# Where the split weights of a hybrid decoder layer lie in SBUF: 128 bytes past a 2048-byte multiple, or on it

## The reference, cut to what matters

```python
h = _rmsnorm(x, norm_gain)
proj = h @ w_in                        # (256, 4096) @ (4096, 15416)
(m_q, m_k, m_v, m_o, m_z, m_i, m_f, a_q, ck, cv, sk, sv, wk, wv, a_gate, a_z) = split(proj)
y_m = mlstm(silu(conv(m_q, m_k)), m_v, m_i, m_f) * sigmoid(m_o) ... * silu(m_z)
y_a = nsa(a_q, ck, cv, sk, sv, wk, wv, a_gate, compressor weights, rel_bias) * silu(a_z)
x = x + concatenate([y_m, y_a]) @ w_out      # (256, 4096) @ (4096, 4096)
return _rmsnorm(x, final_norm_gain)
```

## The kernel before, in words

| tile | before, first byte | modulo 2048 |
|---|---|---|
| `lhs_hi`, `lhs_lo` | 16,512 and 49,280 | 128 |
| `w_raw` (16 KiB) | 82,048 | 128 |
| `w_split` (32 KiB) | 98,432 | 128 |
| arena (88,320 bytes; all tiles made by `at`) | 131,200 | 128 |
| `c128` (constants, 444 columns: identity, masks) | 219,520 | 384 |

## Time and profile before

### The profile page before, as it was taken

How to read it: one execution, slowest core, us unless ns; L and a number is a source line. 1 busy time by engine, 2 the same in 40 slices (tenths; PEclk the granted TensorE clock), 3 DMA queues, 4 the chain that set the end, 5 groups by cost and what they waited for, 6 DMA issues and landing times.

```text
span 1848.8 us, 24131 instructions
## 1 busy us (share of the span) xinstructions
PE 1820.6 (98%) x8488; PEld 1511.8 (82%) x8488; DVE 1141.1 (62%) x1461; ACT 828.7 (45%) x1120; POOL 77.1 (4%) x54
## 2 busy tenths in 40 slices
PE   7999999999999999999999999999999999999997
PEld 6878888888888888888888888888888888888886
DVE  4544644467676676876666666756675775455554
ACT  5534444444454444434444444444443544444443
POOL 0000000000101010010000000000000000000000
PEclk9999999999999999999999999999999999999999
DMA  7676555544545444445555556555655566666664
GB/s 266 184 198 208 194 190 192 193 160 149 181 147 171 158 159 160 152 167 172 193 193 188 177 193 193 185 181 194 192 184 181 172 217 237 205 205 204 205 203 172
DMA packets 100266, 345.62 MB, mean 187 GB/s; under 512 B 10932, under 2 KB 16052, under 8 KB 100052
## 3 DMA queue, kind: packets, MB, share of 16 engines
q1 hardware_dynamic: 93448, 332.68, 54.1%
q10 hardware_dynamic: 6736, 11.77, 2.6%
HBM read 337.07 MB, written 7.33 MB: 186 GB/s over the span
## 4 chain that ended last, share of the span: by engine, by line
PE 95%; DMA 2%; ACT 1%; DVE 1%; issue 0%; SPq 0%; POOL 0%; ACTq 0%; DVEq 0%; POOLq 0%
PE acc_a L441 15%; PE acc_b L441 15%; PE acc_a L443 14%; PE acc_a L442 14%; PE acc_b L443 14%; PE acc_b L442 14%; PE bank_v L448 1%; DMA w_raw<-in_w_all 1%; PE bank_z L689 1%; DMA toe_dram<-toe_row 1%; PE bank_x L443 1%; PE bank_x L442 1%; PE bank_x L441 0%; ACT w_split L843 0%; PE bank_v L449 0%
## 5 line engine op out<-in xcount | busy, mean ns | idle before, releaser
L1206 DVE TENSOR_TENSOR w_split<-w_raw,w_split 128x1024 fp32r<-128x1024 f32 x620 | 777.1, 1255 | 599.2 <-ACT w_split L843 596.1
L843 ACT ACTIVATE w_split<-w_raw 128x1024 fp32r<-128x1024 f32 x620 | 655.3, 1059 | 848.9 <-PE acc_a L443 415.2
L441 PE MATMUL acc_a<-w_split,lhs_hi 128*128 128x512 f32 x1216 | 483.3, 397 | 3.2 <-DVE lhs_lo L1275 3.2
L441 PE MATMUL acc_b<-w_split,lhs_hi 128*128 128x512 f32 x1216 | 479.4, 394 | 0.3 <-issue 0.3
L443 PE MATMUL acc_a<-w_split,lhs_lo 128*128 128x512 f32 x1216 | 474.7, 390 | 0.0
L442 PE MATMUL acc_a<-w_split,lhs_hi 128*128 128x512 f32 x1216 | 474.6, 390 | 0.0
L443 PE MATMUL acc_b<-w_split,lhs_lo 128*128 128x512 f32 x1216 | 473.7, 390 | 0.0
L442 PE MATMUL acc_b<-w_split,lhs_hi 128*128 128x512 f32 x1216 | 473.6, 389 | 0.0
L441 PEld LDWEIGHTS acc_a<-w_split,lhs_hi 128*128 128x128 f32 x1216 | 229.0, 188 | 49.2 <-DVE lhs_lo L1275 2.4
L443 PEld LDWEIGHTS acc_a<-w_split,lhs_lo 128*128 128x128 f32 x1216 | 228.7, 188 | 48.7
L443 PEld LDWEIGHTS acc_b<-w_split,lhs_lo 128*128 128x128 f32 x1216 | 228.3, 188 | 48.1
(11 more groups left out here) (274 smaller groups left out, 927.0 us busy)
## 6 DMA issues: line engine op xcount, KB each, us to landing
w_raw<-in_w_all SPq DMA_DIRECT2D x616, 512.0 KB
wide<-in_x SPq DMA_DIRECT2D x8, 512.0 KB, 10.1
xres<-in_x ACTq DMA_DIRECT2D x8, 512.0 KB, 4.3
out_y<-wide SPq DMA_DIRECT2D x8, 512.0 KB, 3.2
toe_dram<-toe_row ACTq DMA_DIRECT2D x4, 766.0 KB, 10.2
toe<-toe_dram ACTq DMA_DIRECT2D x4, 512.0 KB, 4.6
gain_f<-in_final_norm_gain ACTq DMA_DIRECT2D x1, 2048.0 KB, 14.2
w_raw<-in_w_all SPq DMA_DIRECT2D x4, 224.0 KB
```

The costliest lines, as they stand in the source:

```text
L441: pe.matmul(dst, a[0], b[0], start=start, stop=False)
L843: act.activation(w_hi[:, cols], w_raw[:, cols], ACT.Copy).then_inc(hi_done, 1)
L1206: dve.tensor_tensor(w_lo[:, cols], w_raw[:, cols], w_hi[:, cols].bitcast(F32), ALU.subtract).then_inc(lo_done, 1)
```

## The change

A helper `align(n)` is added, which puts an unused tile behind the last one, large enough that the next begins at a multiple of n bytes. `c128` moves from behind the arena to the place behind `lhs_lo`; then comes the gap; then `w_split`; and `w_raw` goes from in front of `w_split` to behind it. No instruction is added, removed or reordered.

```diff
+        def align(n):
+
+            base = (nc.sbuf_base + 31) // 32 * 32
+            if base % n:
+                sb(f"gap_{base}", (n - base % n) // 4)
...
         lhs_lo = sb("lhs_lo", KT_IN * T, F32R)[:, :].rearrange("p (k t) -> p k t", t=T)
-        w_raw = sb("w_raw", RING * 2 * BW)
-
+        c128 = sb("c128", const128.shape[1])
+        align(4 * BW)
         w_split = sb("w_split", 2 * RING * 2 * BW, F32R)[:, :].rearrange("p (s c) -> p s c", s=2)
         w_hi, w_lo = w_split[:, 0], w_split[:, 1]
+        w_raw = sb("w_raw", RING * 2 * BW)
...
-        c128 = sb("c128", const128.shape[1])
         ident = c128[:, 0:P]
```

## The result

The changed kernel takes 1885.75 us as the median of 4 runs (1883.68 to 1887.36), the kernel before 1851.62 us beside it. The ratio is 1.0175, 95% interval 1.0161 to 1.0190. The range of the prediction ended at 1860 us.

The account below looks back on a forecast made before the run. PE's own pace was taken as the bound, 7296 wide matmuls at 226.9 ns each. All terms were taken as 0: 1850.58 + 0 = 1850.6 us, as a median 1852.8 us, range 1842 to 1860 us.

Parts of the forecast that it names:

- the 2.4 us allowed: Weight transfers on the chain, 24.3 us together: a tenth on each would be 2.4 us up or down; taken as 0.
- take the gain back: If the chain's second weight transfer ended earlier, the `toe_dram` copy behind it would take most of the gain back.
- Rival C: DVE's splits grow beyond their 76% slack and PE waits in the attention: +38 us, 1891 us; chance 0.02.
- the rows nearest in kind: Attention matmuls streaming 512 columns, group 0 without and group 3 with 2048-byte crossings, both 0.23 to 0.24 us: term 0.
- T2: Theory of the follow-up experiments: PE's pace hangs on the first byte of the moving operand; slow case 232 ns, 1886 us.
- T1: Theory of the follow-up experiments, the same as Rival B: PE's pace hangs on the distance between its two operands.
- sign for B: In the output projection, a distance over 227.4 ns between starts of PE's matmuls would make Rival B right.
- Rival B: PE's stationary and moving operands no longer share a remainder: +8.1 ns per wide matmul, +59 us, 1912 us; chance 0.06.
- the rows at 235 ns: The slowest steady 512-column rows of PE in the trace, used as the worst case: +8.1 ns per wide matmul.
- Rival A: PE's pace hangs on the moving operand's first byte: up to 13.6 ns per wide matmul back, -99 us, 1754 us; chance 0.10.
- the unexplained 13.6 ns: Part of each 226.9 ns wide-matmul distance beyond 213.3 ns for 512 columns at one a cycle; 99 us in all.

Follow-up runs that it names:

- the layout at 160: The kernel before with a gap of 160 bytes in front of `w_raw`, `lhs` at 128 and the rest at 288 modulo 2048: 1900.82 us, ratio 1.0255.
- the runs with PE alone: Programs without the layer or other engines' work beside PE's stream, 96 matmuls per case, operand addresses or column counts varied: 226.7 ns at equal remainders (128 x 512 columns).
- the first program: Not the layer: PE alone, 22 cases of 96 matmuls of 512 columns with different operand first bytes; 226.7 ns at difference 0, 232.4 or 233.3 at 128.

## Why the prediction was wrong

**Right: what bounds the kernel, and where an edit of addresses could act.** PE's pace over 7296 wide matmuls is where the whole change is.

**Right: the other engines.** DVE's split is at 1224 ns and ACT's at 1046 ns in the fullest stretch, as against 1225 and 1058; the transfer on the chain at 95.62 takes 11.02 us as against 11.85, inside the 2.4 us allowed. The other one, 12.48 us at 9.77, has no counterpart: the chain of the changed kernel runs over PE's matmuls there. The piece behind the second, `toe_dram<-toe_row` (which writes `toe_dram`; the prediction calls it a copy out of it), takes 9.45 us as against 9.82, so it did not take the gain back; with one execution of each, no more can be said. Rival C did not come.

**Wrong: "I take 0, since the rows nearest in kind, with and without the crossing, agree."** The measurement in it was sound, and is still so in the changed kernel: crossing a 2048-byte multiple costs nothing, and neither does a different first byte. The case that the prediction's last line named as the untested one, a moving operand that begins exactly on a multiple of 2048, is fast too as long as `lhs` begins on one (1851.26 and 1851.90 us). But in every row that I compared, both operands of PE lay in the same relation: `q` and `k` lie a multiple of 256 bytes apart, so do `mv` and `sw`, and `w_split` and `lhs`. Those rows varied the first byte and held fixed the one thing that the change altered. They could answer T2 and were blind to T1. The term came out at +5.4 ns per wide matmul (mean of the distances up to 245 ns over the layer: 232.7 against 227.3), 37 us in the sum of all distances, where I had 0. The prediction's own sign for B, a distance over 227.4 ns, is met in every block.

**Rival B had the mechanism and a fair size.** Its price, 8.1 ns from the rows at 235 ns, was 1.5 times the 5.4 ns measured; 1912 us was forecast for it and 1886 measured. What made me give it 0.06 was this step: "`lhs` slices begin at four different multiples of 512 from matmul to matmul and the distance is the same throughout". That holds but proves nothing, since the relation repeats every 256 bytes: all multiples of 512 are one and the same case. An argument from "it varies and nothing happens" has to vary the quantity by something other than its possible periods. With `lhs` left in place and the weights moved by 1920 bytes, 7.5 times 256, the one relation that all fast rows share was the only thing the trace could not vouch for; the range should have held B's end.

**Rival A's hope** that the unexplained 13.6 ns could come back has nothing left for it among the layouts tried: for 512 columns the best of 16 differences is the one that the kernel before has, and 13.3 ns remain in it. The Trainium skill (TensorE: Matmul & The Clock Gate, section "Wait — 56ns, not 53.3ns?") gives N / 2.4 GHz plus about 2.5 ns, which is 215.8 ns for 512 columns. No fp32r case here reached it: 226.7 ns was the least.

**Open.** Why the difference counts is not settled. Two reads of PE that meet would fit, but this is argued and not shown: the pace depends on the addresses of both operands, repeats every 256 bytes, needs no other engine, and changes with the number of stationary columns too, though not steadily. One more sign is in the traces of the layer. Where the granted clock was 0.50, the 1.2 GHz level (119.4 to 122.4 us in the kernel before, 122.5 to 129 us in the layout at 160), two wide matmuls in a row stand equally far apart at a difference of 0 (the first two rows) and of 160 (the last two):

```profile
121.45 0.63 PE L442 MATMUL acc_a<-w_split,lhs_hi 128*128 128x512 f32 x1
121.88 0.63 PE L443 MATMUL acc_a<-w_split,lhs_lo 128*128 128x512 f32 x1
...
122.72 0.63 PE L450 MATMUL acc_a<-w_split,lhs_hi 128*128 128x512 f32 x1
123.15 0.63 PE L451 MATMUL acc_a<-w_split,lhs_lo 128*128 128x512 f32 x1
```

0.43 us each, 426 or 427 ns by the starts in ns, where 512 columns at one a cycle of 1.2 GHz are 426.7. In these stretches neither the 13.3 ns nor the loss by address shows. The Trainium skill (SBUF — State Buffer, section "SBUF: two separate sides") says that PE never waits on anyone for its ports; the runs with PE alone don't contradict this for other engines, but show that its own two operands are not independent in their addresses. Which structure has the period of 256 bytes, no run here shows. Only this kind of matmul, fp32r with a new stationary operand for each, was tried.

## What to carry to other kernels

When PE's pace is the bound and its work is fp32r matmuls of 128 stationary and 384 or 512 moving columns, place the stationary and the moving tiles at the same remainder modulo 256 bytes, and move them together or not at all (with 256 moving columns or 32 stationary ones a difference of 128 was no loss, so measure there); read the pace from the starts of consecutive matmuls, since a few ns there show in no busy share. Alignment of one operand to a round number is worth nothing by itself: the kernel before was fast with every tile 128 bytes off. Before a row of the trace is taken as the natural experiment for an edit, list what else the edit changes relative to other tiles, and check that the row varies that.

## What the runs showed that I had not expected

- The distance between fp32r matmuls of 512 columns (128 stationary ones) depends on the difference of the operands' addresses modulo 256: 226.7 ns at 0, 236.7 ns at 240, and 237.2 ns at 4 bytes (a case of the first program).
- At equal remainders there is a fixed 13.3 ns per matmul over the columns at 2.4 GHz, for 256, 384 and 512 columns alike. With 256 columns a difference of 128 bytes was faster, 118.6 ns against 120.0.
- At the 1.2 GHz level neither of the two shows: 0.43 us from one wide matmul to the next at a difference of 0 and of 160 bytes.
- A shorter stationary load did not help: 16 to 96 columns gave 228.9 to 231.7 ns against 226.7 with 128.
- A moving fp32r operand read with a step of two elements costs twice the time: 451.1 ns.
